# Order of the high and low products in the wide early blocks of a fused attention and expert layer

## The reference, cut to what matters

```python
q = (h @ peer_wq) ...; s1, s2 = q1 @ sub_keys1.T, q2 @ sub_keys2.T
v1, i1 = top_k(s1, 16); v2, i2 = top_k(s2, 16)      # 8 heads
top_s, pos = top_k(v1[..., None] + v2[..., None, :], 16)
eid, gate = ..., softmax(top_s)                     # 128 chosen experts a token, of 16384
a = gelu(einsum('td,tkd->tk', h, peer_u[eid]))
out = einsum('tk,tkd->td', gate * a, peer_v[eid])
```

## Time and profile before

| | |
|---|---|
| Median of 3 runs | 944.98 us (943.74 to 945.27) |
| The profiled execution | 942.8 us, of which the span on the core 941.0 us |
| TensorE busy (PE) | 932.4 us, 99% |
| VectorE busy (DVE) | 770.6 us, 82% |
| ScalarE busy (ACT) | 500.3 us, 53% |
| GpSimd busy (POOL) | 321.2 us, 34% |
| Granted TensorE clock | 1.000 over the span |
| L2051, high matmuls of wide blocks | 688, 387 to 404 ns each |
| L2048, low matmuls of wide blocks | 688, 276 to 292 ns each |

### The profile page before, as it was taken

How to read it: one execution, slowest core, us unless ns; L and a number is a source line. 1 busy time by engine, 2 the same in 40 slices (tenths; PEclk the granted TensorE clock), 3 DMA queues, 4 the chain that set the end, 5 groups by cost and what they waited for, 6 DMA issues and landing times.

```text
span 941.0 us, 15375 instructions
## 1 busy us (share of the span) xinstructions
PE 932.4 (99%) x5396; PEld 816.7 (87%) x5396; DVE 770.6 (82%) x1450; ACT 500.3 (53%) x872; POOL 321.2 (34%) x292
## 2 busy tenths in 40 slices
PE   9999999999999999999999999999999999999998
PEld 8998899998988888888888888888888888888887
DVE  5899758999886888788778898888888888777776
ACT  6576544433767777777777544334343343343342
POOL 3084228888476766767667000000000000000000
PEclk9999999999999999999999999999999999999999
DMA  9543138826776676667667777787777777766664
GB/s 293 160 135 123 48 99 300 211 78 179 216 245 198 206 218 195 226 195 236 203 200 224 250 246 232 245 242 236 245 236 243 239 237 245 206 219 186 195 193 140
DMA packets 93783, 193.46 MB, mean 206 GB/s; under 512 B 8449, under 2 KB 59265, under 8 KB 93457
## 3 DMA queue, kind: packets, MB, share of 16 engines
q1 hardware_dynamic: 93280, 190.38, 64.8%
q0 software_dynamic: 288, 2.10, 1.2%
q10 hardware_dynamic: 144, 0.08, 0.0%
HBM read 174.43 MB, written 15.99 MB: 202 GB/s over the span
## 4 chain that ended last, share of the span: by engine, by line
PE 95%; ACT 2%; DVE 2%; DMA 1%; issue 0%; DVEq 0%; ACTq 0%
PE psum L2131 37%; PE psum L2051 16%; PE psum L2048 8%; PE psum L1675 5%; PE psum L1975 5%; PE psum L1944 4%; PE psum L2111 4%; PE psum L2077 3%; PE psum L2045 2%; PE psum L1691 2%; PE psum L2114 2%; PE psum L1732 1%; PE psum L1853 1%; PE psum L1969 1%; PE psum L1936 1%; DMA up_kept<-gel 1%
## 5 line engine op out<-in xcount | busy, mean ns | idle before, releaser
L2131 PE MATMUL psum<-rr 128*128 128x512 f32 x1536 | 354.0, 390 | 1.0 <-DVE rr L1399 1.0
L2131 PEld LDWEIGHTS psum<-rr 128*128 128x128 f32 x1536 | 286.0, 188 | 64.6 <-issue 1.1
L851 ACT ACTIVATE rr<-raw 128x1024 fp32r<-128x1024 f32 x105 | 111.7, 1064 | 176.4 <-PE psum L2131 176.2
L1332 DVE TENSOR_TENSOR rr<-raw,rr 128x1024 fp32r<-128x1024 f32 x106 | 129.9, 1225 | 25.9 <-ACT rr L851 25.5
L2051 PE MATMUL psum<-h_all,rr 128*128 128x512 f32 x456 | 123.4, 395 | 0.0
L2051 PEld LDWEIGHTS psum<-h_all,rr 128*128 128x128 f32 x456 | 82.5, 188 | 13.5
L1352 DVE TENSOR_REDUCE gel<-psum 128x256 f32<-128x512 f32 x86 | 58.6, 681 | 14.3 <-DMA up_kept<-gel 12.7
L759 ACT ACTIVATE rr<-raw 128x1024 fp32r<-128x1024 f32 x64 | 67.2, 1050 | 4.7 <-DMA raw<-in_peer_u_dram 4.6
L2051 PE MATMUL psum<-h_all,late_b 128*128 128x512 f32 x232 | 64.8, 394 | 0.0
L1635 POOL TENSOR_TENSOR rr<-raw,h_all 128x640 fp32r<-128x640 bf16 x32 | 40.3, 1259 | 59.0 <-DVE raw L1309 58.7
L1399 DVE TENSOR_TENSOR rr<-big,rr 128x256 fp32r<-128x256 f32 x128 | 54.4, 425 | 4.4
(11 more groups left out here) (240 smaller groups left out, 1766.5 us busy)
## 6 DMA issues: line engine op xcount, KB each, us to landing
raw<-in_peer_v_dram SPq DMA_DIRECT2D x128, 512.0 KB, 3.9
raw<-in_peer_u_dram SPq DMA_DIRECT2D x127, 512.0 KB, 4.2
up_kept<-gel SPq DMA_DIRECT2D x106, 128.0 KB, 3.6
gel<-up_kept SPq DMA_DIRECT2D x106, 128.0 KB, 3.9
big<-in_w_in_dram SPq DMA_DIRECT2D x10, 1024.0 KB, 5.7
big<-in_peer_wq_dram SPq DMA_DIRECT2D x8, 1024.0 KB, 5.5
big<-in_w_out_dram SPq DMA_DIRECT2D x4, 1024.0 KB, 5.3
rr<-big POOLq DMA_DIRECT2D x2, 1024.0 KB, 8.9
```

Source lines behind the costliest of these rows:

```text
L851: act.activation(v_sp[b % 2][:, 0, :], early_v(b), ACT.Copy).then_inc(v_hi, 1)
L1332: dve.tensor_tensor(v_sp[b % 2][:, 1, :], early_v(b), f(v_sp[b % 2][:, 0, :]), ALU.subtract).then_inc(v_lo, 1)
L2131: i = pe.matmul(psum[:, 4 + 2 * t + n, :], g_sp[:, s, x, t * P:(t + 1) * P], v_sp[s][:, y, n * 512:(n + 1) * 512], start=(first and m == 0 ...
```

## The change

The split of a wide block's 24 units changes; the matmuls, their operands and their number stay. Before, highs stand at the even units 0 to 12 (k = 0 to 6), lows at units 14 to 21 (k = 0 to 7), and the last high (k = 7) at unit 22. After, the units with a matmul are

- high: 0, 2, 5, 8, 11, 14, 17 and 22 for k = 0 to 7,
- low: 4, 7, 10, 13, 16, 19, 20 and 21 for k = 0 to 7,

so the order is H0 H1 L0 H2 L1 H3 L2 H4 L3 H5 L4 H6 L5 L6 L7 H7. The wait for the low part stands ahead of unit 4 in a wide block, and no longer ahead of unit 14.

```diff
@@ -110,6 +110,8 @@
 FIRST_NEXT = SPLIT_E[1]
+HIGH_AT = {(0 if k == 0 else 3 * k - 1 if k < DK - 1 else UNITS - 2): k for k in range(DK)}
+LOW_AT = {(3 * k + 4 if k < DK - 2 else UNITS - 4 + k - (DK - 2)): k for k in range(DK)}
 WIDE = (FILL0 + 6, EARLY - 2)
@@ -2038,16 +2040,16 @@
-                    if n == (2 * DK - 2 if wide(e) else 2 * DK):
+                    if n == (4 if wide(e) else 2 * DK):
                         split_low_ready(pe, e)
                     bank = psum[:, early_bank(e), :]
                     if not wide(e):
                         i = pe.matmul(bank[:, 0:SEQ], early_split(e, x)[:, k, :], ht[:, y, k, :], start=(n == 0), stop=(n == UNITS - 1))
-                    elif 2 * DK - 2 <= n < UNITS - 2:
-                        k = n - (2 * DK - 2)
+                    elif n in LOW_AT:
+                        k = LOW_AT[n]
                         i = pe.matmul(bank[:, 0:SEQ], early_split(e, 1)[:, k, :], ht[:, 0, k, :], start=False, stop=False)
-                    elif n % 2 == 0:
-                        k = n // 2 if n < 2 * DK else DK - 1
+                    elif n in HIGH_AT:
+                        k = HIGH_AT[n]
                         i = pe.matmul(bank.rearrange("p (a t) -> p a t", a=2), early_split(e, 0)[:, k, :], ht[:, :, k, :],
                                       start=(k == 0), stop=(k == DK - 1))
```

## The result

| | before | after |
|---|---|---|
| Median of 6 runs each | 944.68 us (943.43 to 945.35) | 948.94 us (945.19 to 949.97) |
| Ratio | | 1.0039, 95% interval 1.0026 to 1.0052 |
| Profiled execution, its span | 942.8, 941.0 us | 945.19, 943.4 us |
| Start of wide block 20 | 255.42 us | 255.17 us |
| From there to the last wide high matmul | 268.59 us | 271.98 us |

The changed kernel is slower by 0.39%; the medians themselves lie 4.3 us (0.45%) apart.

What follows compares the result with a forecast made beforehand. TensorE was taken as the bound, busy for 266.00 of 266.00 us in the gate stage. Stalls 4.27 + pushes 0.5 - order 0.9 = +3.9 us, on 944.98 us gives 948.9 us; range 945.6 to 952.5.

Steps and rivals of the forecast that it cites:

- The order gives 0.9 us: Wide blocks: alternating highs and lows saves 0.01 us a block, times 86 blocks, 0.9 us off.
- The moved wait stalls TensorE at GpSimd's low parts alone: Gate stage: low part wanted 0.46 us into the block, not 1.62; only even blocks, GpSimd's, are late.
- The 0.22 us behind a low part: Delay from the low part's end to the first low matmul, read at block 46 and used in every stall sum.
- the list of thirteen: The wide blocks forecast to be late, all even, of 86 examined; their stalls sum to 7.3 us.
- A group costs its largest stall: Late low parts keep their clock times within a group: 0.86 + 1.18 + 1.10 + 1.13 = 4.27 us.
- the walk back: Following each late low part back through previous instructions or releasers; between anchors it never met TensorE.
- The term of 0.5 us for pushes: Allowance over all groups for low parts pushed along by TensorE's delay, four times a piece like 0.12 us.
- The group of blocks 58 to 78, 1.10 us: Late blocks 58, 64, 70, 72 and 78, paced from the copy at 363.73; largest stall 1.10 us, in block 72.
- One slip is enough: Rival: TensorE falls behind once and later low parts are in time; 945.3 us, up to 946.8; chance 0.17.
- the three copies: ScalarE's copies of gate sums at 282.30, 363.73 and 454.37, the anchors where it waits for TensorE and groups begin.
- Every late block pays: Rival: low parts are pushed along with TensorE, +7.3 us and nothing from the order; 952.3 us; chance 0.15.
- The order speeds TensorE up: Rival: alternation lowers the pitch; at a 2.71 us block it gives 2.1 us, 942.9 us; chance 0.05.

Runs made afterwards that it cites:

- the early wait without the alternation: Order of the kernel before, with the wait for the low part ahead of unit 4: 947.6 us against 943.78, ratio 1.0039.
- the odd blocks: Alternation and early wait in odd wide blocks alone, even ones as in the kernel before: 943.29 us, ratio 0.9994.
- the wait at unit 0: Order of the kernel before, with the wait for the low part ahead of unit 0: 950.29 us against 944.3, ratio 1.0062.
- profile 1: First profile of the changed kernel, the fastest of its six runs: profiled execution 945.19 us, span 943.4 us, stalls 4.04 us.
- the even blocks: Alternation and early wait in even wide blocks alone, odd ones as in the kernel before: 947.33 us, ratio 1.0041.
- the kernel with VectorE first by a wait: Changed kernel plus a wait: GpSimd's second gated product of step 16 waits for VectorE's low part of block 61; 947.34 us against 944.24 before.
- the wait at unit 8: Order of the kernel before, with the wait for the low part ahead of unit 8: 946.33 us, ratio 1.0018.
- the two kernels with a list: Changed kernel with listed blocks kept as before: thirteen late ones, 943.89 us against 944.24; those plus 21, 26 and 73, 943.99 against 944.3.
- profile 2: Changed kernel run once more for a second profile: 947.66 us, ratio 1.0037, profiled span 945.6 us, stalls 5.48 us.
- the last kernel above: Changed kernel, but the thirteen late blocks and 21, 26 and 73 keep the old order and wait: 943.99 us against 944.3, ratio 1.0.

## Why the prediction was right, step by step

- *The number.* +3.9 us was forecast; the medians differ by 4.3 us and the ratio gives 3.7. The mechanism is right, but so close a hit is partly luck: several terms below were off, some up and some down.
- *The order gives 0.9 us.* Right in kind, a third too much. The median block went from 2.800 to 2.793 us, 0.6 us over the stage. The forecast read 0.01 us from one block and the loop. A high pitch and a low pitch add up to nearly the same in both orders.
- *The moved wait stalls TensorE at GpSimd's low parts alone.* Shown twice: the early wait without the alternation makes the loss, the odd blocks do not.
- *Which blocks, and how much.* The number for block 20 was met, 0.86 us, by two errors that cancel. The 0.22 us behind a low part was read at block 46, where TensorE was busy with its highs until 338.43 and could not have come sooner; the stalls of both profiles give about 0.16. And the low part of block 20 ended 1.16 us into the block instead of 1.10. Outside the list of thirteen only block 26 stalled, for 0.05 us; of the thirteen, block 70 stalled in neither profile, and 64 and 78 only in the second. The single sums did not hold inside a group, and were not meant to: block 46 was forecast to pay 1.18 less the 0.83 already paid at block 38, 0.35, and paid 0.18 and 0.27.
- *A group costs its largest stall.* In the main right (the wait at unit 0). In detail the first group paid 1.42 us where 1.18 + a push of 0.12 was forecast; the excess is block 52, which paid 0.46 and 0.33 where nothing was forecast. The prediction looked for a push between blocks 38 and 46. There was next to none: from the profile of before to profile 1 the low part of block 46 ends 0.24 us later, while TensorE comes 1.21 us later. That of block 52 ends 1.67 us later, and the two profiles part at VectorE's low part and GpSimd's product ahead of it. First before, then profile 1:
```profile
343.55 1.23 DVE L1325 TENSOR_TENSOR rr<-raw,rr 128x1024 fp32r<-128x1024 f32 x1 [0.33 <-ACT rr L759]
...
343.66 2.25 POOL L1635 TENSOR_TENSOR rr<-raw,picks 128x640 fp32r<-128x640 bf16 x1
```
```profile
344.16 2.29 DVE L1327 TENSOR_TENSOR rr<-raw,rr 128x1024 fp32r<-128x1024 f32 x1 [0.67 <-ACT rr L761]
...
344.12 1.25 POOL L1637 TENSOR_TENSOR rr<-raw,picks 128x640 fp32r<-128x640 bf16 x1
```
  VectorE, 0.11 us ahead before, is now 0.04 us behind, and ends 1.67 us later: 0.61 us for its later start, 1.06 for the lost turn. It is the same exchange as at block 64. GpSimd is first here in five traces (both of the changed kernel, the early wait in the order of before, the even blocks, and the kernel with VectorE first by a wait), and the low part of block 52 ends 0.61 to 0.78 us into the block. VectorE is first in five (before, the odd blocks, the wait at unit 8, and the two kernels with a list), and it ends 0.36 us into the block or earlier. So the step that failed for block 52 is the walk back, which took the turns of the two engines as fixed. The term of 0.5 us for pushes came out at the right size by luck: 1.42 us in the first group and 1.27 in the last (without block 104) against 1.18 and 1.13.
- *The group of blocks 58 to 78, 1.10 us.* Wrong in kind. It pays 0.24 or 1.75 us, by which of two engines is first at one instruction. The forecast read the low part of block 72 from one execution and took it as fixed. That 1.10 lies between the two is luck. The profiled spans are 2.4 and 4.6 us over that of before.
- *The end of the stage.* The wait ahead of the first down product shrank from 0.96 to 0.44 us in profile 1, which hides the stall of 0.33 us in block 104, as forecast. In profile 2 it grew to 1.27 us instead and hid nothing:
```profile
536.20 0.47 PE L2133 MATMUL psum<-rr 128*128 128x512 f32 x1 [1.27 <-DVE rr L1401]
```
- *What would show it.* The waits came as described, eleven with a longest of 1.0 us. TensorE's busy time was to fall by 3 to 4 us; it fell by 1.3 of the 268 us from 258 to 526 us:
```profile
258.00:526.00 268.00, 266.73 (x1595) 234.52 (x1594) 217.90 (x245) 194.47 (x402) 178.81 (x100) 1.00 0.67 210
```
  That was wrong by the overlap of modelled ends, which takes 0.28 us of each stall in the matmul rows and not 0.16, so that a stall under about 0.3 us leaves no trace there (the rows of the loads show it). Block 20, with the largest stall, lies ahead of 258 us. The first down product was to start at 535 us or so, and started at 534.1 and 536.2.
- *Rivals.* "One slip is enough" falls with the waits that remain at the three copies, and with the stalls in blocks 96 and 98. "Every late block pays" falls with the wait at unit 0. "The order speeds TensorE up" falls with the block of 2.793 us.

Open: why single executions of one kernel lie up to 5 us apart, more than the 1.5 us which the one exchange ahead of block 64 explains. Block 20 varied too, 0.86 to 1.25 us. Three executions stand out from their sets with a mean granted clock of 0.998: 948.87 us for the kernel before (4.6 us over its median), 950.03 for the even blocks and 946.67 for the last kernel above (2.7 us over each). The profile of the wait at unit 0 shows what such a drop costs, 1.6 us; the other three have no profile, and other long executions of the changed kernel, such as that of 949.75 us, ran at 1.000.

## What to carry to other kernels

A reordering on the engine that bounds a kernel changes next to nothing by itself if its instructions cost the same in either order, but it moves the first use of each operand. So compare when each operand is ready with when the new order wants it, one by one, in the timeline; averages of busy time show room where single deadlines have none. Then ask for each late one what paces it: where the helpers keep their own pace, delays do not add up and only the largest counts, until the helpers wait for the bound engine again. Look also for two helpers that start work within some tenths of a microsecond of each other and slow each other down: there the order can turn, and the time read from one execution does not hold for the next.

## What the runs showed of the hardware that was not expected

When two instructions of VectorE and GpSimd run beside each other here, the one that started first keeps its full speed (VectorE 1.22 us, or GpSimd 1.25 us), and the other one takes 2.29 (GpSimd) or 2.08 us (VectorE). The second ends 1.11 or 1.08 us after the first, so they rather take turns than share. A lead of 0.03 or 0.04 us was enough. In the gate stage of all thirteen traces, GpSimd's gated product takes 1.25 to 1.29 us where it started ahead of VectorE's low part (188 times) and 2.23 to 2.29 us where that had started first (120 times). So a DMA that lands 0.3 us later can turn the order round, and the chain behind it moves by a whole microsecond. The Trainium skill, "Advanced Engine Details and Errata", section "GPSIMD Details", says that the two engines share a read and a write interface when VectorE has two SBUF inputs. That fits these rows, in which VectorE's low part reads two such inputs.

A stall can cost more than its own length. After 2.33 us of idle time at block 20 in the wait at unit 0, the granted clock was 0.51 from 259 to 262 us, and the matmuls ran at half their pace for 3.4 us. In the other twelve profiles TensorE's longest idle time in this stage was 1.3 us, and the granted clock stayed at 1.00 through it. That the idle time caused the drop is not shown by an experiment.
